# Moving one branch's output products into the sparse attention, and pairing the table products, in a two-block transformer kernel

## What is computed

```python
y_a = dsa_sparse_attention(a_q, a_k, a_v, i_q, i_k, i_w, positions, rel_bias)   # 8 heads of 64, top-k keys
y_b = mla_attention(q_nope, q_rope, k_nope, k_rope, v_b)                        # 8 heads of 64
gates = sigmoid(g + b_gate)
merged = gates[:, :, 0] * (y_a @ w_branch_a) + gates[:, :, 1] * (y_b @ w_branch_b)
x = x + merged @ w_out
# inside the sparse attention, per head:
logits = q @ k_sel.T * 64 ** -0.5 + rel_table[rel_bucket(pos_q - pos_k)]        # bias by bucket of distance
```

## Time and profile before

| what | us |
|---|---|
| median of the timed runs (3) | 2272.43 |
| lowest and highest of them | 2269.82, 2281.14 |
| the profiled execution | 2278.02 |
| its span in the profile | 2276.2 |
| TensorE busy in it | 2177.5 (96%) |
| VectorE busy | 1346.6 (59%) |
| ScalarE busy | 872.3 (38%) |

### The profile page before, as it was taken

The page is one execution under the profiler, slowest core; times in us unless marked ns, Lnnn a source line. Parts: engine busy times, 40 slices in busy tenths (PEclk is TensorE's granted clock), DMA queues, the critical chain, the costliest instruction groups (busy, mean ns, idle before and its releaser), DMA issues.

```text
span 2276.2 us, 26336 instructions
## 1 busy us (share of the span) xinstructions
PE 2177.5 (96%) x10663; PEld 1698.4 (75%) x10665; DVE 1346.6 (59%) x2279; ACT 872.3 (38%) x1453; POOL 154.5 (7%) x101
## 2 busy tenths in 40 slices
PE   5999999999999998999999999999899999999998
PEld 4755888888877966687877887777564588888886
DVE  7697468847835476457654665557773364633632
ACT  4355434424423255434422432333364433422421
POOL 0463100000010000010000001000000001000000
PEclk9999989999999999989999999999896799999999
DMA  8342226565432210103333333122021032333331
GB/s 299 123 152 85 75 71 207 191 198 177 152 96 65 75 56 29 47 29 98 102 102 103 93 99 107 55 84 84 27 76 65 10 93 84 100 95 96 98 93 65
DMA packets 67113, 225.03 MB, mean 99 GB/s; under 512 B 7216, under 2 KB 8112, under 8 KB 66992
## 3 DMA queue, kind: packets, MB, share of 16 engines
q1 hardware_dynamic: 64112, 218.11, 30.2%
q10 hardware_dynamic: 2880, 5.24, 0.6%
HBM read 215.98 MB, written 7.34 MB: 98 GB/s over the span
## 4 chain that ended last, share of the span: by engine, by line
PE 87%; DVE 7%; ACT 3%; issue 2%; DMA 0%; POOL 0%; SPq 0%; DVEq 0%; POOLq 0%; ACTq 0%
PE bank L290 23%; PE bank L292 23%; PE bank L291 23%; PE bank L295 17%; PE bank L795 2%; DVE wlo L330 1%; ACT whi L317 1%; DVE tmp L524 1%; DVE Hl L529 1%; ACT pr L768 1%; DVE sc L2051 0%; DVE steps L2049 0%; DVE pr L760 0%; DMA XT<-in_xT 0%; POOL small L504 0%
## 5 line engine op out<-in xcount | busy, mean ns | idle before, releaser
L290 PE MATMUL bank<-Hh,whi 128*128 128x512 f32 x1632 | 652.6, 400 | 30.8 <-DVE wlo L330 7.4
L291 PE MATMUL bank<-Hl,whi 128*128 128x512 f32 x1632 | 643.4, 394 | 0.0
L292 PE MATMUL bank<-Hh,wlo 128*128 128x512 f32 x1632 | 643.3, 394 | 0.0
L330 DVE TENSOR_TENSOR wlo<-stg,whi 128x1024 fp32r<-128x1024 f32 (+1 forms) x299 | 358.8, 1205 | 424.2 <-ACT whi L317 423.7
L317 ACT ACTIVATE whi<-stg 128x1024 fp32r<-128x1024 f32 (+1 forms) x309 | 313.7, 1025 | 462.0 <-PE bank L292 454.4
L290 PEld LDWEIGHTS bank<-Hh,whi 128*128 128x128 f32 x1632 | 310.9, 190 | 105.7 <-issue 9.3
L292 PEld LDWEIGHTS bank<-Hh,wlo 128*128 128x128 f32 x1632 | 311.1, 191 | 66.7
L291 PEld LDWEIGHTS bank<-Hl,whi 128*128 128x128 f32 x1632 | 311.2, 191 | 62.5 <-issue 0.2
L290 PE MATMUL bank<-HIDh,whi 128*128 128x512 f32 x352 | 145.7, 414 | 0.0
L292 PE MATMUL bank<-HIDh,wlo 128*128 128x512 f32 x352 | 141.1, 401 | 0.0
L291 PE MATMUL bank<-HIDl,whi 128*128 128x512 f32 x352 | 140.0, 398 | 0.0
(11 more groups left out here) (290 smaller groups left out, 2848.3 us busy)
## 6 DMA issues: line engine op xcount, KB each, us to landing
raw<-in_mod_w SPq DMA_DIRECT2D x96, 512.0 KB, 4.2
stg<-in_ffn_in SPq DMA_DIRECT2D x88, 512.0 KB, 4.2
stg<-in_ff SPq DMA_DIRECT2D x64, 512.0 KB, 3.6
stg<-in_ffn_out SPq DMA_DIRECT2D x40, 512.0 KB, 3.7
stg<-in_cm_w SPq DMA_DIRECT2D x24, 512.0 KB, 3.8
stg<-in_gates SPq DMA_DIRECT2D x16, 512.0 KB, 3.5
stg<-in_z_ch SPq DMA_DIRECT2D x12, 512.0 KB, 3.6
bias_kept<-out_b ACTq DMA_DIRECT2D x20, 256.0 KB, 2.1
```

The costliest lines, as they stand in the source:

```text
L290: pe.e.matmul(out_, l[0], r[0], start=start, stop=False, skip_group_check=True)
L291: pe.e.matmul(out_, l[0], r[1], start=False, stop=False, skip_group_check=True)
L292: return pe.e.matmul(out_, l[1], r[0], start=False, stop=stop, skip_group_check=True)
L330: hand.e.tensor_tensor(wlo[j % NW][:, 0:n * c], stg[j % NSTG][:, 0:n * c], whi[j % NW][:, 0:n * c].bitcast(F32), ALU.subtract).then_inc(*m ...
```

## The change

Three things.

1. The blocks of `br_b` stand before those of `br_a` in the plan. The products of `br_b` are issued by a generator that goes on by one step after each turn of `dsa`, from turn 8: six products (two K tiles of one result tile) at each of sixteen turns, into banks 4 and 5. VectorE's generator splits the weights and multiplies the results with their gates; ScalarE's splits the weights. `dsa` has three banks for scores and one for the transposes. After it only `br_a` is left, and each of its result tiles is merged at once.
2. The table products are issued two steps at a time, at every second call, and begin two calls later.
3. `table_dve` moves out of `bias_dve` to the end of the rotation generator, which goes on once per block during the MLP's input product.

```diff
--- before.py
+++ after.py
@@ -129,9 +129,8 @@
     for j in range(4):
         plan.append(("w_uq", 0, 2, 256 * j, 256))
         plan.append(("w_uk", 0, 1, 128 * j, 128))
-    for j in range(4):
-        gemm("br_a", 0, 4, [256 * j])
-        gemm("br_b", 0, 4, [256 * j])
+    gemm("br_b", 0, 4, range(0, D, 256))
+    gemm("br_a", 0, 4, range(0, D, 256))
     gemm("w_out", 0, DT, range(0, D, 256))
     for a, b in FF2_CHUNKS:
         gemm("ff1", 0, DT, range(128 * a, 128 * b, 256))
@@ -1841,6 +1840,7 @@
                 dve.e.tensor_scalar(a1[R2, :], a2[R2, :], cst[R2, C_A:C_A + 1], cst[R2, C_B:C_B + 1], ALU.mult, ALU.add).then_inc(
                     *dve_done.up("turned"))
                 yield
+                table_dve("ds", 16, td, tt_, Tb)
 
             def scalar():
                 for _ in range(11):
@@ -1863,11 +1863,13 @@
             STEPS = 4 * FIRST[4]
 
             def bias_pe():
-                for u in range(-4, STEPS):
-                    if u >= 0:
-                        b = BIAS_BANKS[u // 4 % 2]
-                        if u % 4 == 0:
-                            open_bank(b, [(act_done, ("ds", "bias", u // 4))])
+                for _ in range(6):
+                    yield
+                for first in range(0, STEPS, 2):
+                    b = BIAS_BANKS[first // 4 % 2]
+                    if first % 4 == 0:
+                        open_bank(b, [(act_done, ("ds", "bias", first // 4))])
+                    for u in (first, first + 1):
                         pe.wait_ge(*dve_done["ds", "step", u])
                         for x in range(4):
                             g = 4 * (u % 4) + x
@@ -1875,9 +1877,10 @@
                                 tok = mm(banks[b][:, 32 * g:32 * g + 32], step8[:, u % 8, x * P:(x + 1) * P], Tb[:, y, :], y == 0, y == 2)
                         tok.then_inc(*core_done.up(("ds", "step", u)))
                     yield
+                    yield
 
             def bias_act():
-                for m in range(-2, FIRST[4]):
+                for m in range(-3, FIRST[4]):
                     if m < 0:
                         for _ in range(4):
                             yield
@@ -1894,7 +1897,6 @@
                         yield
 
             def bias_dve():
-                table_dve("ds", 16, td, tt_, Tb)
                 for qb in range(4):
                     for u in range(4 * FIRST[qb], 4 * FIRST[qb + 1]):
                         c = 4 * (u - 4 * FIRST[qb])
@@ -2087,7 +2089,54 @@
 
             mla = Core("mla", [mla_item(2 * j + n // 4, n % 4) for j in range(4) for n in range(8)], [0, 1, 2], [3], sq,
                        SC + [RB], stat_b, 1)
-            dsa = Core("dsa", [dsa_item(h, qb) for qb in range(4) for h in range(H)], [0, 1, 2, 5], [3, 4], sq, SC + [ROT], stat_a, 1)
+            dsa = Core("dsa", [dsa_item(h, qb) for qb in range(4) for h in range(H)], [0, 1, 2], [3], sq, SC + [ROT], stat_a, 1)
+
+
+            HOST = 8
+
+            def branch_b_pe():
+                for _ in range(HOST):
+                    yield
+                for j in range(4):
+                    jb = next_block(pe, "br_b", 0)
+                    hi, lo = block_parts(jb)
+                    for m in range(2):
+                        tile = (("bb", j), m)
+                        into, c = acc_bank(tile, [(dve_done, ("mb", 2 * j + m))]), slice(m * P, (m + 1) * P)
+                        pe.wait_ge(*lo_done(jb))
+                        for q in range(4):
+                            pe.wait_ge(*dve_done["yb", q])
+                            tok = mm3(into[:, :], (hi[:, q, c], lo[:, q, c]), (YBh[:, q, :], YBl[:, q, :]), q == 0, q == 3)
+                            if q == 3:
+                                tok.then_inc(*gemm_done.up(tile, *([("block", jb)] if m else [])))
+                            if q % 2:
+                                yield
+
+            def branch_b_act():
+                for _ in range(HOST):
+                    yield
+                for j in range(4):
+                    next_block(act, "br_b", 0)
+                    for _ in range(4):
+                        yield
+
+            def branch_b_dve():
+                for _ in range(HOST + 1):
+                    yield
+                for j in range(4):
+                    next_block(dve, "br_b", 0)
+                    for t in (2 * j, 2 * j + 1):
+                        yield
+                        yield
+                        dve.wait_ge(*gemm_done[("bb", j), t % 2])
+                        dve.wait_ge(*act_done["gate", 8 + t])
+                        dve.e.tensor_tensor(GT[:, 8 + t, :], GT[:, 8 + t, :], bank((("bb", j), t % 2))[:, :], ALU.mult).then_inc(
+                            *dve_done.up(("mb", t)))
+
+            def both(core, other):
+                for _ in core:
+                    next(other, None)
+                all_of(other)
 
             def lead_mla(heads):
                 def lead(i):
@@ -2240,12 +2289,12 @@
                     mm3(b[:, :], (CQh[:, 2, c], CQl[:, 2, c]), (hi[:, 0, :], lo[:, 0, :]), True, True).then_inc(
                         *gemm_done.up(("uv", tb), *([("block", j)] if tb == 3 else [])))
                 all_of(mla.tensor(None, lead_mla(heads_pe)))
-                all_of(dsa.tensor())
+                rotate_banks([4, 5])
+                both(dsa.tensor(), branch_b_pe())
+                rotate_banks([0, 1, 2, 3, 4])
                 for j in range(4):
                     gemm(("ba", j), "br_a", lambda q: (YAh[:, q, :], YAl[:, q, :], dve_done["ya", 6 + q // 2]), 0, 4, 1,
                          lambda m, j=j: [(dve_done, ("ma", 2 * j + m))])
-                    gemm(("bb", j), "br_b", lambda q: (YBh[:, q, :], YBl[:, q, :], dve_done["yb", q]), 0, 4, 1,
-                         lambda m, j=j: [(dve_done, ("mb", 2 * j + m))])
                 gemm("out", "w_out", lambda q: (MGh[:, q, :], MGl[:, q, :], dve_done["mg", q]), 0, DT, 4,
                      lambda m: [(dve_done, ("x", "f2", m))])
 
@@ -2295,7 +2344,7 @@
                 dve.wait_ge(*dve_done["sel", 3])
                 all_of(mla.vector(mla_close_dve, lead_mla(heads_dve)))
                 split_b_dve(3)
-                all_of(dsa.vector(dsa_close_dve))
+                both(dsa.vector(dsa_close_dve), branch_b_dve())
                 split_a_dve(7)
 
                 def a_evac(t):
@@ -2303,12 +2352,6 @@
                     dve.wait_ge(*act_done["gate", t])
                     dve.e.tensor_tensor(GT[:, t, :], GT[:, t, :], bank((("ba", t // 2), t % 2))[:, :], ALU.mult).then_inc(
                         *dve_done.up(("ma", t)))
-
-                def b_evac(t):
-                    dve.wait_ge(*gemm_done[("bb", t // 2), t % 2])
-                    dve.wait_ge(*act_done["gate", 8 + t])
-                    dve.e.tensor_tensor(GT[:, 8 + t, :], GT[:, 8 + t, :], bank((("bb", t // 2), t % 2))[:, :], ALU.mult).then_inc(
-                        *dve_done.up(("mb", t)))
                     dve.wait_ge(*dve_done.now)
                     dve.e.tensor_tensor(GT[:, t, :], GT[:, t, :], GT[:, 8 + t, :], ALU.add).then_inc(*dve_done.up(("merged", t)))
                     dve.wait_ge(*act_done["mgh", t])
@@ -2317,7 +2360,6 @@
 
                 for j in range(4):
                     beside_gemm(dve, "br_a", 0, 4, 1, a_evac, 2 * j)
-                    beside_gemm(dve, "br_b", 0, 4, 1, b_evac, 2 * j)
 
                 def x_evac(m):
                     dve.wait_ge(*gemm_done["out", m])
@@ -2367,7 +2409,7 @@
                     act.e.activation(VB[:, tb, :], bank(("uv", tb))[:, :], ACT.Copy).then_inc(*act_done.up(("vb", tb)))
                 all_of(mla.scalar(mla_close_act, lead_mla(heads_act)))
                 split_b_act(3)
-                all_of(dsa.scalar(dsa_close_act))
+                both(dsa.scalar(dsa_close_act), branch_b_act())
                 split_a_act(7)
 
                 def merged(t):
@@ -2375,11 +2417,10 @@
                     act.e.activation(MGh[:, t, :], GT[:, t, :], ACT.Copy).then_inc(*act_done.up(("mgh", t)))
 
                 for j in range(4):
-                    beside_gemm(act, "br_a", 0, 4, 1)
-                    beside_gemm(act, "br_b", 0, 4, 1, merged, 2 * j)
+                    beside_gemm(act, "br_a", 0, 4, 1, merged, 2 * j)
 
                 def x_act(m):
-                    scale_high("f2", m, vcol("mlp_norm_g_2", 0, 8), gemm_done[("bb", 3), 1])
+                    scale_high("f2", m, vcol("mlp_norm_g_2", 0, 8), gemm_done[("ba", 3), 1])
                     square("f2", m, x_tile(m), dve_done["x", "f2", m])
 
                 beside_gemm(act, "w_out", 0, DT, 4, x_act)
@@ -2415,9 +2456,8 @@
                 bias_in(2)
                 sp.wait_ge(*dve_done["dsa", "soft", 7, 0])
                 bias_in(3)
-                for j in range(4):
-                    beside_gemm(sp, "br_a", 0, 4, 1)
-                    beside_gemm(sp, "br_b", 0, 4, 1)
+                beside_gemm(sp, "br_b", 0, 4, 4)
```

(1 more changed line is left out.)

## The result

The changed kernel takes 2240.4 us (median of 4 runs, 2235.8 to 2244.8) against 2273.8 us (median of 4, 2269.8 to 2281.1) on the same chip: a ratio of 0.985 (95% interval [0.982, 0.988]), 33 us less. Forecast were 26.7 us less, 2246 us. The profiled execution ran 2241.6 us with a span of 2239.8, against 2278.0 and 2276.2.

What follows compares the result with a forecast made beforehand. TensorE was taken as the bound, at half clock in the sparse attention. Gains of 21.0 us (clock) and 7.3 (tables), less 0.6 (banks) and 1.0 (merges), made 26.7, so 2246 us, range 2235 to 2262.

Steps and rivals of the forecast that it cites:

- The clock under the attention: Sparse attention: sixteen turns at full clock gain 25.1 us, less 2.5 until the rise and 1.6 for visits: 21.0.
- The precedent: In the attention just before, the clock rose from 0.50 within 3 us of similar products; attention turns then held 1.00.
- The turns: Sparse attention: turns 9 to 23 were to take 2.7 to 3.6 us each.
- Banks: Sparse attention: fewer banks for scores and turns cost 0.6 us (0 to 2), in small first turns and last four.
- Merges: First branch's products after the attention: VectorE's merging of result tiles becomes slower than TensorE, 1.0 us lost (0 to 5).
- Tables: Table products: start's stall, its after-effect, fewer visits and the end gain 7.3 us together (3 to 8).
- The start: Table products: TensorE's 2.5 us stall before the first step goes, and 1.25 us of after-effect comes back.
- Pairs and tail: Table products: fewer visits gain 3.2 us (0 to 4), and the end gains 0.4.
- The third rival: Branch move works; tables bring only the start's stall, or the merges cost 5 us: 2252 us, chance 9%.
- The second: Attention's clock rises late or falls again, or VectorE and ScalarE hold TensorE back: 2257 us, chance 14%.
- The fourth: Attention's gain is whole, the rise immediate, no losses at banks or merges: 2240 us, chance 10%.
- The first: Sparse attention's clock stays at 0.50 through the visits, so the kernel is slower: +16, 2288 us, chance 7%.

Runs made afterwards that it cites:

- burst12: Kernel before with the new banks and twelve unread full-size products, six after each of turns 8 and 9 of the sparse attention: 2250.2 us, 0.989.
- unpaired: Changed kernel with the table products issued one step a visit, the early small table kept: 2245.7 us, 0.985 of the kernel before.
- filler16: Kernel before with the new banks and six unread full-size products after each of turns 8 to 23 of the sparse attention: 2276.7 us, 1.000.
- filler16_rows64: filler16 with its unread products cut to 64 of the 128 rows: 2320.0 us, 1.020 of the kernel before.
- host2: Changed kernel with the first branch visit after turn 2 instead of turn 8: 2233.3 us, 0.982 of the kernel before.
- move_only: Kernel before with only the branch move, its banks and its merges, the tables as before: 2250.1 us, 0.989.
- host2_warm: host2 with 26 unread full-size products in TensorE's wait at the start of mla: 2231.8 us, 0.979 of the kernel before.
- whole_change: The changed kernel timed once more beside the kernel before: 2242.3 us, 0.985.
- copies_early: Changed kernel with ScalarE's copies of the bias two calls earlier: 2242.3 us, 0.984 of the kernel before.

## Why the prediction was right

The mechanism was the forecast one. The time, 2240.4 us, lies 0.6 us below the forecast's band of 2241 to 2251 and inside the range of 2235 to 2262. By its steps, each difference taken between the two profiles:

- **The clock under the attention.** 25.1 less 2.5 and 1.6 made 21.0 us. With 96 products moved in, the sixteen turns of the earlier trace rows were to take 57.3 - 25.1 + 21.9 + 2.5 + 1.6 = 58.2 us; they took 57.2. The rise was mis-sized: taken at 5 us after the first visit, it came after 2.3, and the first visit took 2.51 us where a later one takes 1.50 (1721.84 to 1723.34), so 1.0 us was lost and not 2.5. The visits take back 0.5: sixteen of 1.50 us are 24.0, where 21.9 + 1.6 = 23.5 were worked out. The turns alone came out as worked out: in burst12 the sixteen from 1730.18 to 1763.87, less its second visit of 1.50 us, take 32.2. That the rise came at 2.3 us is luck, though. It isn't a fixed time: 8 us in unpaired with the same attention and 8 to 9 in filler16 lie near the other bound of what was allowed for (0 to 10), and in unpaired that made the stretch 3.0 us longer.
- **The precedent.** The prediction took the rise at 1650.90 for the work of the products that began at 1648.17. The runs above, where the same mla rose before it reached them, show that this needn't be so; and from 1667.42 on such products stand in the row that was read as attention turns alone (1660 to 1670). The reading turned out right for the sparse attention by filler16 and burst12, not by this precedent.
- **The turns.** Those of 256 keys take 2.96 us (1720.38 to 1723.34), inside 2.7 to 3.6; those of 384 keys rise to 3.89, above it:

```profile
1760.74 0.34 PE L294 MATMUL bank<-Msel,identb 128*128 128x384 bf16 x1
...
1764.63 0.34 PE L294 MATMUL bank<-Msel,identb 128*128 128x384 bf16 x1
```

- **Banks.** 0.6 us forecast. From the first score product to the first visit 12.9 us against 12.5 (1717.25 to 1729.72): 0.4, in the small turns as said:

```profile
1707.20 0.23 PE L294 MATMUL bank<-Msel,identb 128*128 128x128 bf16 x1 [0.55 <-DVE stat_a L759]
```

- **Merges.** 1.0 us forecast, none measured: the output product starts right behind the last product of br_a. The estimate put the eighth tile 0.3 us late with a period of 7.2; at 6.9 to 7.0 it is in time.
- **Together** the attention stretch gave 21.7 us (140.4 to 118.7) where these steps made 25.1 - 2.5 - 1.6 - 0.6 - 1.0 = 19.4.
- **Tables.** 7.3 us forecast, 6.6 measured. The start was to bring 2.5 + 1.25 = 3.75 and brought 3.9. Pairs and tail were to bring 3.6 and brought 2.7. The price of a visit held: two steps now come every 3.51 us, against 2 x 1.80. Of the 0.9 that lack, 0.5 are the longer waits for ScalarE's copies, for which the forecast had 0.3; the other 0.4 are not located. VectorE's wait of 1.21 in the earlier trace rows is gone.
- **The third rival** is out (the tables brought more than the stall). **The second** is out: no fall after the rise. **The fourth** names the measured time, 2240, but not by its reasons: the banks and the rise did cost something. **The first** is out in the changed kernel and is what filler16_rows64 shows.

Attention and tables make 28.3 of the 36.4 us by which the two profiles differ. The other 8 us lie in code that the change hardly touches: 3.2 before the table stretch (1149.8 against 1146.6 us), 1.7 between the tables and mla, 0.7 in mla, and 2.5 from the output product to the end. The same code gave other lengths in other runs: the piece from the output product to the next MLP's is 137.3 us in before, filler16 and host2, 135.7 in after, move_only and host2_warm, and mla goes with the time of the rise, as said. The medians, too, differ by more than the two parts: by 33 and 34 us in the two timings of the change, against 28. Whether the lower clock there is chance or follows from when the run gets there stays open; no run separates it. So the forecast's steps account for 28 us, about 2245 and in its band; the last 5 us are none of its doing.

What the experiments corrected is the reason, not the number. The prediction leaned on a visit in every turn to hold the clock; after two visits the turns held it by themselves.

## What to carry to other kernels

Where a full TensorE sits at half its granted clock, look at the kind of its products before moving work: try a dozen unread full-size products at the start of the stage, which took 4.4 us here and, these included, left the stage 21 us shorter, and only then decide whether real work is worth scheduling there. Place them before the first small or gappy turns, or in the wait itself, so that the clock doesn't fall at all. Price a move by what the same instructions take at either level in the trace, and don't take a full engine as proof that the clock will rise. Compare stages over several profiles before a difference of a few microseconds is put down to an edit: the rise alone moved one by 3 us under the same instructions.

## What the runs showed of the hardware that was not expected

- What went before decided the clock of a full engine: the same attention turns ran 58 us at 0.50 in the kernel before and, after twelve full-size products, to the end of the stage at 1.00 (burst12; the banks differ, but with the new banks and products of 64 rows it stayed at 0.50).
- 96 products with 64 of 128 rows in 16 visits didn't lift it: 0.50 throughout the visits, 2320.0 us. With 128 rows it was up behind the first visit of six in burst12, behind the second in filler16.
- The time to the rise isn't fixed: 2.1 to 3.1 us after the first visit in the profiles of four kernels (whole_change, copies_early, after, move_only) and 8 in that of unpaired, with the same instructions.
- 26 products that nobody reads, in a wait of 7.6 us, kept the clock at 1.00 where it had been 0.50, and mla became 1.6 us shorter (host2_warm against host2); the medians can't tell the two apart.
